# Fewer fillers per step at the end of the first attention, two more steps that carry them, and the turns of heads two steps later

## The reference

```python
h = _rmsnorm(x, attn_pre_norm[l])
qkv = h @ w_qkv[l]
# differential head: two maps, one v of 128
logits = einsum('bhmqd,bhmkd->bhmqk', q, k) * scale + bias      # masked below the diagonal
w = softmax(logits)[:, :, 0] - lam * softmax(logits)[:, :, 1]
diff_o = _rmsnorm(w @ v, diff_subln) * (1 - lam_init)
# stick-breaking head, v of 64
log_1mb = where(strict, log_sigmoid(-z), 0)
between = cumsum(log_1mb, reverse=True) - log_1mb
sb_o = _rmsnorm(where(strict, exp(log_sigmoid(z) + between), 0) @ v, sb_norm)
mix = concatenate([diff_o, sb_o]) @ w_o[l]
x = x + _rmsnorm(mix, attn_post_norm[l])
```

## Time and profile before

| | |
|---|---|
| median of three runs | 1667.31 us (1667.16 to 1668.07) |
| profiled execution, own time | 1668.98 us |
| span of its trace | 1667.2 us |
| PE busy | 1635.2 us (98%) |
| DVE, ACT, POOL busy | 692.5, 684.6, 753.7 us |
| mean granted TensorE clock | 0.996 |

### The profile page before, as it was taken

One profiled execution on the slowest core, in us unless ns is written; L12 is line 12 of the kernel. 1 busy time (PEld: TensorE's weight loads), 2 busy tenths in 40 slices (PEclk: granted clock), 3 DMA queues, 4 the chain that ended last, 5 costly groups with the idle time before them and its releaser, 6 DMA issues.

```text
span 1667.2 us, 21229 instructions
## 1 busy us (share of the span) xinstructions
PE 1635.2 (98%) x8088; PEld 1349.0 (81%) x8088; DVE 692.5 (42%) x1395; ACT 684.6 (41%) x1204; POOL 753.7 (45%) x574
## 2 busy tenths in 40 slices
PE   9999999999999999999999999999999999999997
PEld 7777778888888887888888888888778888888885
DVE  6176664884444226312212225555673311112224
ACT  5366655543334324422223234566573422223322
POOL 7424325574445552744444553543113554444550
PEclk9999999999999999999999999999999999999999
DMA  5411102232232231323223222212002232222231
GB/s 202 146 51 51 39 14 101 102 101 91 99 102 90 99 101 51 123 93 101 97 92 101 95 96 101 89 65 77 26 26 89 89 101 95 95 101 92 98 101 51
DMA packets 42117, 147.37 MB, mean 88 GB/s; under 512 B 4768, under 2 KB 5152, under 8 KB 42016
## 3 DMA queue, kind: packets, MB, share of 16 engines
q1 hardware_dynamic: 40536, 143.13, 25.4%
q10 hardware_dynamic: 1480, 2.89, 0.5%
HBM read 142.84 MB, written 3.41 MB: 88 GB/s over the span
## 4 chain that ended last, share of the span: by engine, by line
PE 91%; DVE 3%; ACT 3%; issue 2%; DMA 1%; POOL 1%; DVEq 0%; ACTq 0%; POOLq 0%
PE PS L492 20%; PE PS L493 20%; PE PS L494 20%; PE PS L1059 5%; PE PS L1070 5%; PE PS L467 4%; PE PS L891 4%; PE PS L867 3%; PE PS L474 2%; PE PS L882 2%; PE PS L514 1%; PE PS L516 1%; PE PS L515 1%; DVE L L975 1%; POOL w_lo L536 0%
## 5 line engine op out<-in xcount | busy, mean ns | idle before, releaser
L536 POOL TENSOR_TENSOR w_lo<-stage,w_hi 128x512 fp32r<-128x512 f32 x524 | 709.5, 1379 | 843.5 <-ACT w_hi L524 842.5
L524 ACT ACTIVATE w_hi<-stage 128x1024 fp32r<-128x1024 f32 x262 | 274.7, 1057 | 509.1 <-DMA stage<-in_weights 508.9
L492 PE MATMUL PS<-H_hi,w_hi 128*128 128x512 f32 x992 | 387.7, 391 | 0.4 <-DVE rcol L1249 0.4
L494 PE MATMUL PS<-H_hi,w_lo 128*128 128x512 f32 x992 | 385.9, 389 | 0.0
L493 PE MATMUL PS<-H_lo,w_hi 128*128 128x512 f32 x992 | 385.9, 389 | 0.0
L492 PEld LDWEIGHTS PS<-H_hi,w_hi 128*128 128x128 f32 x992 | 186.2, 188 | 40.3 <-issue 1.0
L493 PEld LDWEIGHTS PS<-H_lo,w_hi 128*128 128x128 f32 x992 | 186.2, 188 | 39.5 <-issue 1.0
L494 PEld LDWEIGHTS PS<-H_hi,w_lo 128*128 128x128 f32 x992 | 186.2, 188 | 38.6
L492 PE MATMUL PS<-A_hi,w_hi 128*128 128x512 f32 x528 | 205.6, 389 | 0.3 <-DVE A_lo L646 0.2
L493 PE MATMUL PS<-A_lo,w_hi 128*128 128x512 f32 x528 | 205.4, 389 | 0.0
L494 PE MATMUL PS<-A_hi,w_lo 128*128 128x512 f32 x528 | 205.4, 389 | 0.0
(11 more groups left out here) (214 smaller groups left out, 2063.0 us busy)
## 6 DMA issues: line engine op xcount, KB each, us to landing
stage<-in_weights SPq DMA_DIRECT2D x262, 512.0 KB, 3.2
out_t<-Y SPq DMA_DIRECT2D x8, 256.0 KB, 2.0
X<-in_x_t SPq DMA_DIRECT2D x3, 512.0 KB, 8.3
bias_line<-bias_line ACTq DMA_DIRECT2D x1, 1270.0 KB
strip<-bias_line ACTq DMA_DIRECT2D x1, 1024.0 KB, 5.0
stage<-in_weights SPq DMA_DIRECT2D x2, 256.0 KB, 4.5
X<-in_x_t ACTq DMA_DIRECT2D x2, 256.0 KB, 6.0
V<-QF SPq DMA_DIRECT2D x4, 128.0 KB, 2.3
```

What stands on the lines that cost most here:

```text
L492: pe.matmul(out, a, h_hi, start=first, stop=False, skip_group_check=skip)
L494: return pe.matmul(out, b, h_hi, start=False, stop=last, skip_group_check=skip)
L524: act.activation(w_hi[:, slot, :], stage[:, slot, :], ACT.Copy).then_inc(hi_done, 1)
L536: lo = pool.tensor_tensor(w_lo[:, slot, cols], stage[:, slot, cols], w_hi[:, slot, cols].bitcast(F32), ALU.subtract)
```

## The change

Only the table `FILL1` differs.

```diff
-FILL1 = ([7] * 8 + [8] * 4) * 2 + [7] * 8 + [8] + [6] * 8
-FILL1 = FILL1 + [(0, 4)] * 2 + [(3, 4)] * 4 + [(3, 0), (3, 12), (12, 6), 6]
+FILL1 = ([7] * 8 + [8] * 4) * 2 + [7] * 8 + [6] * 4 + [5] * 4 + [4] * 3
+FILL1 = FILL1 + [(0, 4)] * 2 + [(3, 4)] * 4 + [(3, 12), (12, 6)]
```

## The result

| | before | changed |
|---|---|---|
| median | 1668.3 us (10 runs) | 1671.3 us (10 runs, 1670.28 to 1674.49) |
| ratio | | 1.0018, 95% interval 1.0009 to 1.0026 |
| profiled execution | 1668.98 us, span 1667.2 | 1670.51 us, span 1668.7 |

The changed kernel is 3 us (0.18%) slower, at the top end of the range I gave, twice what I forecast (+1.5). One of before's ten executions took 3287 us: the ratio leaves it out, the median of 1668.3 holds it (1668.07 for the nine others). The page is of one of the ten executions of the changed kernel.

A forecast was written before the change was run, and what follows sets the result against it. It took a loop over PE, ACT and DVE to bound steps 36 to 44, and PE's work what follows. +0.3 at full clock and +1.2 for a dip gave +1.5, a median of 1668.8 us, range 1666.1 to 1671.3.

The forecast's parts named there:

- What bounds the kernel: Steps 36 to 44 are set by a loop over PE, ACT and DVE; what lies behind by PE's work.
- The path from step 40 to 42: Product of step 40 to that of step 42: length stays 5.99 us, wait 1.3; step 41's fillers win nothing.
- From step 42 to the second turn: DVE sets this path: step 42 starts at 210.36, second turn at 220.96, PE waits about 0.7, 1.7 and 1.8 us.
- Two turns and six matmuls on top, and new waits: Behind the second turn: 2.26 us of PE work on top, plus 1.0 us for three new waits of turns.
- The sum at full clock: End of the first attention's output product at unchanged full clock: -0.70 + 1.0, so 0.3 us later.
- The clock's price in the changed kernel: A clock dip at the same place as before, 215.8 to 222.6, costing +1.2 us.
- The profiled execution: Whole kernel when profiled: +1.5 us on 1668.98, so 1670.5 us.
- Rival B: The dip comes from step 44 on, where PE is the bound: +3.7, 1671.0 us, slower; chance 0.15.
- Rival A: No clock dip in the changed kernel: +0.3, 1667.6 us; chance 0.29.
- Rival C: Fillers fill PE's idle time in steps 41 and 42, before's dip goes: -3.6, 1663.7 us, faster; chance 0.05.

The follow-up runs named there:

- traces with extras: Before and the changed kernel, each with extra 128x128 matmuls on constants ahead of PE's waits in the first attention; stretches of 198.84 and 200.83 us.
- the one timed pair: Timed runs of before and the changed kernel, both with extra matmuls in the first attention alone: 1668.48 and 1669.51 us.
- after_again: The changed kernel, unchanged, run again for a second trace and more timed executions: ratio 1.0027 against before, stretch 204.08 us.

## Why the prediction was right or wrong

**What bounds the kernel: right.** The stretch of steps 36 to 44 is a loop over ACT and DVE. With PE's idle time in before filled up, DVE stays busy for 3.7 to 3.9 of 4 us and the turn of step 44 comes no earlier than 221.87.

**The path from step 40 to 42: right to the hundredth.** Length 5.99, wait 1.28 against 1.32. The fillers of step 41 won nothing. Before that I had 1.15 us gained at the product of step 40; it was 0.90 (205.52 - 204.03 - 0.59): the wait of 0.80 grew by 0.38 instead of 0.23, so 0.36 of 0.46 was left behind it, and the three fillers from there on gave 0.54 instead of 0.69.

**From step 42 to the second turn: right.** Forecast 10.60 us, measured 10.49 (210.02 to 220.51). The waits that I gave as 0.7, 1.7 and 1.8 were 0.67, 1.63 and 0.31; the last is short at least in part because the clock had fallen and PE's work ahead of it had swollen. (My three waits add up to 4.2 us, not to the 4.5 that I called idle.)

**Two turns and six matmuls on top, and new waits: right in sum, not in its terms.** From the turn of step 44 to the end of the output product it was 53.46 us before (223.92 to 277.38) and 56.83 after (220.51 to 277.34): 3.4 us more against 2.26 + 1.0. Of the three new waits two show, 0.21 and 0.24 us, less than half of what I took. In the traces with extras it is 3.05 us more (221.87 to 275.48, 221.22 to 277.88), with waits of 0.23 and 0.24. What makes up the rest, 0.3 to 0.7 us beyond the moved work and these waits, I have not found; a little is the half clock, which lasts 0.5 us past 220.51.

**The sum at full clock: right for one trace, wrong as a base.** "+0.3 at an unchanged full clock" was measured as 200.83 - 200.61 = +0.22. But it sets a changed kernel without a dip against a before with one. Here is the step that failed: I credited before with the whole price of its profiled dip, 1.8 us, as if every execution of before paid it (it stands inside the 2.96 us: the turn at 223.92 where a full clock would have allowed 222.1), and then moved to the median by subtracting 1.67 us. For that one trace the price was right (1.77). But before's second trace paid 0.67 us for a dip of the same length, and the timed runs with extras lie only 0.4 us below those without (1.4 with extras in both attentions). The sum should have set full clock against full clock, +2.0, and added the difference of what dips cost each kernel on average.

**The clock's price in the changed kernel: mis-sized too.** I priced its dip at 1.2 us, from the one place where before's had stood. Its two traces paid 0.33 and 3.25. So my dips came to 1.2 - 1.8 = -0.6 us between the kernels. By the timed runs the changed kernel lies 3.0 and 4.0 us above before (1671.3 against 1668.3, 1672.46 against 1668.45); with 1.9 to 2.0 us of it owed to the order, 1 to 2 us are left for its dips above what before pays for its own (2 to 3 by the 1.03 of the one timed pair). The sign of that term was wrong. That the clock is in it also shows in the changed kernel's ten executions: the three with a mean granted clock of 0.994 took 1672.14 to 1674.49 us, the seven at 0.996 and 0.997 took 1670.28 to 1672.21.

**The profiled execution: luck.** I forecast 1670.5 for it and it took 1670.51. But its parts are not mine: 0.55 us in the touched stretch, where I had 1.5, made up by an attention that began 0.59 us earlier, and 1.5 us of a dip in the second attention that I had not thought of.

Rival B named the mechanism (a dip on the stretch where PE is the bound), with 0.15. after_again comes near it: the clock fell at 218.4, not behind 219.5, and the 3.25 us it cost, close to B's 3.4, came from 10.2 us at half clock, not 6.8. Rival A does not occur in either trace in the first attention. Rival C is refuted: nothing was won in steps 41 and 42, and the kernel is slower.

The rule of the Trainium skill that I weighed ("TensorE: Matmul & The Clock Gate", section "What's actually happening": the monitor runs free of the kernel's start) fits what the traces show: with the same program the clock fell at 215.7 and at 211.2 before, and for 3.4 us from 217.6 and for 10.2 us from 218.4 after. I had set it aside because three times of before lay within 0.9 us. Nine executions of before spread over 2.5 us, and ten of the changed kernel over 4.2. Three times were too few to speak against a rule.

## What to carry to other kernels

Where a loop over several engines sets the pace, a filler moved within that stretch gained nothing here; eight that came out of a stretch where PE is the bound gained their whole 1.9 us, and what left the stretch (two turns and six matmuls) was paid behind it, in full and a little more. When a trace shows a clock dip, price every kernel first at full clock, then ask where in each the thin place ends: a dip under another engine's path cost little here (0.67 of 6.8 us), one in PE-bound work nearly half its length (1.5 of 3.4 us in the second attention). Compare stretches of two traces with their dips listed, never ends of spans, and take the level of a kernel from many executions before subtracting anything seen in one.

## What the hardware showed that I had not expected

In the traces of before and of the changed kernel the clock fell with no idle gap of PE longer than 1.7 us ahead of it: in the first trace of the changed kernel behind 4 us in which PE was busy for 2.37, in the second attention behind 2.42 of 4. In the trace of before the same 2.42 of 4 us in the second attention left it at 1.00. With 16 to 23 small matmuls on constants (some 0.22 us each) put under waits that exist anyway, none of the six traces has a dip in the first attention, and all seven without them have one. No cost of them can be seen: before's product of step 42 starts 134.64 us behind the attention's first with them (211.28 - 76.64) and 134.74 without (211.51 - 76.77).
